# Down layer as seven block products (Strassen's scheme) in four chunks of inner rows

## What is computed

```python
def squared_relu_mlp(h, w_up, w_down):        # h 512x1024, w_up 1024x4096, w_down 4096x1024
    u = jax.nn.relu(h @ w_up)
    return (u * u) @ w_down
...
        h2 = _rms(x, norm2_g[l]).astype(dt)
        x = x + squared_relu_mlp(h2, w_up[l], w_down[l]).astype(dt)
    return x[:, BLOCK:]
```

## Time and profile before

| | us |
|---|---|
| median of 3 runs | 1192.71 (1192.49 to 1193.37) |
| the profiled execution | 1193.66 |
| its span in the trace | 1191.9 |
| PE busy | 1174.0 (98% of the span) |
| DVE, ACT, POOL busy | 499.2, 491.0, 468.1 |

### The profile page before, as it was taken

The page is one execution under the profiler, slowest core; times in us unless marked ns, Lnnn a source line. Parts: engine busy times, 40 slices in busy tenths (PEclk is TensorE's granted clock), DMA queues, the critical chain, the costliest instruction groups (busy, mean ns, idle before and its releaser), DMA issues.

```text
span 1191.9 us, 20669 instructions
## 1 busy us (share of the span) xinstructions
PE 1174.0 (98%) x8782; PEld 963.1 (81%) x8782; DVE 499.2 (42%) x994; ACT 491.0 (41%) x808; POOL 468.1 (39%) x288
## 2 busy tenths in 40 slices
PE   8999999999999999999999999999999999999998
PEld 7998877887798688667777777778888888888887
DVE  4699425454554643442452675262522000222000
ACT  6455423323323534765726544433634221343220
POOL 3443435335343234333323622343444544344541
PEclk9999999999999999999999999999999999999999
DMA  6222323122222152212522312342223332222330
GB/s 252 89 71 89 108 90 108 57 86 97 90 73 73 36 164 67 65 36 73 193 75 67 106 53 64 107 148 71 88 89 102 111 106 89 78 99 94 118 124 36
DMA packets 35998, 111.47 MB, mean 94 GB/s; under 512 B 4273, under 2 KB 9137, under 8 KB 35394
## 3 DMA queue, kind: packets, MB, share of 16 engines
q1 hardware_dynamic: 30288, 98.59, 24.9%
q10 hardware_dynamic: 5106, 11.43, 2.7%
q0 software_dynamic: 512, 0.13, 0.1%
HBM read 99.43 MB, written 9.04 MB: 91 GB/s over the span
## 4 chain that ended last, share of the span: by engine, by line
PE 83%; DVE 8%; ACT 4%; POOL 2%; issue 2%; DMA 0%; DVEq 0%; ACTq 0%
PE pst L1856 19%; PE pst L1858 18%; PE pst L1857 17%; PE pst L2032 5%; PE pst L2031 5%; PE pst L2030 5%; POOL w_lo L818 1%; PE pst L2371 1%; ACT w_hi L936 1%; PE pst L2363 1%; PE pst L2096 1%; PE pst L2149 1%; PE pst L2348 1%; PE pst L2333 1%; DVE cdif L1418 1%
## 5 line engine op out<-in xcount | busy, mean ns | idle before, releaser
L818 POOL TENSOR_TENSOR w_lo<-raw,w_hi 128x1024 fp32r<-128x1024 f32 x164 | 401.9, 2455 | 632.4 <-ACT w_hi L936 620.7
L1856 PE MATMUL pst<-h_hi,w_hi 128*128 128x512 f32 (+1 forms) x704 | 257.1, 365 | 1.3 <-DVE h_lo L1391 0.7
L1858 PE MATMUL pst<-h_hi,w_lo 128*128 128x512 f32 (+1 forms) x704 | 243.3, 346 | 0.0
L1857 PE MATMUL pst<-h_lo,w_hi 128*128 128x512 f32 (+1 forms) x704 | 242.9, 345 | 0.0
L936 ACT ACTIVATE w_hi<-raw 128x1024 fp32r<-128x1024 f32 x164 | 172.1, 1054 | 140.2 <-PE pst L2032 114.1
L1856 PEld LDWEIGHTS pst<-h_hi,w_hi 128*128 128x128 f32 x704 | 133.4, 189 | 25.9 <-issue 5.4
L1857 PEld LDWEIGHTS pst<-h_lo,w_hi 128*128 128x128 f32 x704 | 133.6, 190 | 15.7 <-issue 2.9
L1858 PEld LDWEIGHTS pst<-h_hi,w_lo 128*128 128x128 f32 x704 | 133.3, 189 | 15.9
L1856 PE MATMUL pst<-x_hi,w_hi 128*128 128x512 f32 (+1 forms) x272 | 102.6, 377 | 0.4 <-DVE x_lo L1722 0.4
L1857 PE MATMUL pst<-x_lo,w_hi 128*128 128x512 f32 (+1 forms) x272 | 102.4, 377 | 0.0
L1858 PE MATMUL pst<-x_hi,w_lo 128*128 128x512 f32 (+1 forms) x272 | 102.4, 376 | 0.0
(11 more groups left out here) (339 smaller groups left out, 1991.8 us busy)
## 6 DMA issues: line engine op xcount, KB each, us to landing
raw<-in_weights SPq DMA_DIRECT2D x164, 512.0 KB, 3.3
xt<-in_x SPq DMA_DIRECT2D x4, 512.0 KB, 5.4
wait_gate<-stage ACTq DMA_DIRECT2D x8, 256.0 KB, 2.0
gate_t<-wait_gate ACTq DMA_DIRECT2D x1, 2048.0 KB, 8.8
x<-in_x ACTq DMA_DIRECT2D x1, 2048.0 KB, 7.5
out<-x SPq DMA_DIRECT2D x7, 256.0 KB, 3.9
cst<-in_consts SPq DMA_DIRECT2D x1, 1524.0 KB, 11.3
wait_ret_g<-stage ACTq DMA_DIRECT2D x4, 256.0 KB, 2.2
```

The lines of the kernel that those rows point to most:

```text
L818: nc.gpsimd.tensor_tensor(w_lo[:, u % W_SLOTS, :], raw[:, u % RAW_SLOTS, :], w_hi[:, u % W_SLOTS, :].bitcast(F32), ALU.subtract).then_inc( ...
L1856: M(out, lh, rh, start=(first and i == 0), stop=False)
L1857: M(out, lh, rl, start=False, stop=False)
L1858: last = M(out, ll, rh, start=False, stop=(final and i == len(terms) - 1))
```

## The change

The inner rows are taken in four chunks of eight blocks of 128. In a chunk the down product is a 2x2 by 2x2 block product: the activations are split by tokens (two halves of 256) and by inner rows (two halves of four blocks), w_down's rows of the chunk likewise and its columns in two halves of 512. Seven products of such blocks are computed instead of eight, in the variant with shared partial sums (U11, U12, U22 and the sums S1 to S4 of the activations; four of the seven weight operands are differences). Each product is two jobs of one unit and 12 matmuls of 128x512 into two banks; three pairs of banks are used in turn.

- Units: 56 down units instead of 32; those of differences are raw blocks, loaded again. DVE subtracts another raw buffer from them in place (`weight_sums`, 8 per chunk) before ACT converts them; DVE does it ahead of its own step of an up or down job, for units up to five ahead of the job's. SP's load of a buffer also waits until the last such sum that reads it.
- Raw buffers: three more, so six, from the first up unit on; two lie in the space of constants no longer used.
- Up: ACT's relu goes to `usq`; DVE multiplies it by the relu of the PSUM bank (that empties the bank); ACT copies to `u_hi`, DVE subtracts to `u_lo`; behind each second job (the jobs pair block f with block f+4) DVE forms four sums of 128x256, ACT copies them in one go (128x1024), DVE makes their low parts (128x1024).
- Adding up: after each product DVE adds both banks to their places in `x2`; two of the products go to several quadrants, are collected in `shared` over the first three chunks, and are added to `x2` by `share_out` in the up stage of the last chunk.

In the diff, a line of "..." stands where lines are left out.

```diff
-JOBS = (PHASE_C + PHASE_A + PHASE_B + PHASE_D + PHASE_E + proj_jobs(BRANCH_SW) + PHASE_O + up_jobs(0) +
-        down_jobs(0) + up_jobs(1) + down_jobs(1))
+FC = 8
+NFC = DFF // P // FC
+UP_ORDER = [0, 4, 1, 5, 2, 6, 3, 7]
+TH = T // 2
+
+
+U11, U12, U22, S1, S2, S3, S4 = range(7)
+PRODUCTS = [("p11", U11, (0, 0)), ("p12", U12, (1, 0)), ("p51", S1, (0, 1)), ("p62", S2, (1, 1)),
+            ("p42", U22, (1, 0)), ("p73", S3, (0, 0)), ("p34", S4, (1, 1))]
+LESS = {2: 0, 3: 2, 4: 3, 5: 3}
+GOES_TO = [None, [(0, 0)], [(0, 1), (1, 1)], None, [(1, 0)], [(1, 0), (1, 1)], [(0, 1)]]
+NM = len(PRODUCTS)
+SHARED = {0: [(0, 0), (0, 1), (1, 0), (1, 1)], 3: [(0, 1), (1, 0), (1, 1)]}
+
+
+def up_jobs(c):
+    return [("up", c, i) for i in range(FC)]
+
+
+def down_jobs(c):
+    return [("down", c, (m, j)) for m in range(NM) for j in range(2)]
+
+
+JOBS = (PHASE_C + PHASE_A + PHASE_B + PHASE_D + PHASE_E + proj_jobs(BRANCH_SW) + PHASE_O +
+        [j for c in range(NFC) for j in up_jobs(c) + down_jobs(c)])
...
+        return u
+    (r, q), j = PRODUCTS[u[2][0]][2], u[2][1]
+    return "w_down", 4 * u[1] + 2 * r + j, q
...
+RAW_MORE = 3
+RAW_AT, RAW_FILL, _c = [], [], {}
+for _n in range(NU):
+    _i = (_n - FFN0) % (RAW_SLOTS + RAW_MORE)
+    RAW_AT.append(RAW_SLOTS + _i if _n >= FFN0 and _i < RAW_MORE else _n % RAW_SLOTS)
+    _c[RAW_AT[-1]] = _c.get(RAW_AT[-1], 1 if RAW_AT[-1] >= RAW_SLOTS else 0) + 1
+    RAW_FILL.append(_c[RAW_AT[-1]])
+LESS_UNIT = {UNIT_NO[("w_down", c, (m, j))]: UNIT_NO[("w_down", c, (LESS[m], j))]
+             for c in range(NFC) for m in LESS for j in range(2)}
+SUM_NO = {u: i for i, u in enumerate(sorted(LESS_UNIT))}
+LAST_SUM = {}
+for _u in sorted(LESS_UNIT):
+    LAST_SUM[LESS_UNIT[_u]] = SUM_NO[_u]
...
+        def down_bank(g, t):
+            return [(4, 5), (6, 7), (1, 3)][g % 3][t]
...
+        def operand_split(c, which, p):
+
+            return 3 * (FC // 2 * c + p) + (1 if which == U11 else 2 if which < S1 else 3)
...
             for u in range(RAW_SLOTS, NU):
-                sp.wait_ge(lo_ready, u - RAW_SLOTS + 1)
+                held = u - RAW_SLOTS if u < FFN0 + RAW_MORE else u - RAW_SLOTS - RAW_MORE
+                sp.wait_ge(lo_ready, held + 1)
+                if held in LAST_SUM:
+                    sp.wait_ge(raw_summed, KD + LAST_SUM[held] + 1)
...
-                    act.wait_ge(raw_in[u % RAW_SLOTS], 16 * (u // RAW_SLOTS + 1))
+                    act.wait_ge(*raw_loaded(u))
+                    if u in LESS_UNIT:
+                        act.wait_ge(*sums_done(u))
                     if u >= W_SLOTS:
                         act.wait_ge(dense_done, LAST_JOB[u - W_SLOTS] + 1)
-                    nc.scalar.activation(w_hi[:, u % W_SLOTS, :], raw[:, u % RAW_SLOTS, :], ACT.Copy)\
+                    nc.scalar.activation(w_hi[:, u % W_SLOTS, :], raw_unit(u), ACT.Copy)\
                         .then_inc(hi_ready, 1)
...
                 elif kind == "up":
-                    i = kind_no(n)
-                    if i >= 2:
-                        act.wait_ge(u_lo_ready, i - 1)
-                    A(ub[:, i % 2, :], one, ACT.Relu).then_inc(job_out[kind], 1)
+                    i, p, q = kind_no(n), b // 2, usq[:, b // 2 % 2, b % 2, :]
+                    act.wait_ge(dense_done, n + 1)
+                    if i >= 4:
+                        act.wait_ge(u_lo_ready, 3 * (i // 2 - 1))
+                    A(q, one, ACT.Relu).then_inc(u_hi_ready, 1)
                     act.wait_ge(job_out[kind], i + 1)
-                    if a == 1 and b == 0:
-                        act.wait_ge(dense_done, n)
-                    A(u_hi[:, b, :], ub[:, i % 2, :], ACT.Square).then_inc(u_hi_ready, 1)
+                    if b % 2 == 0:
+                        A(u_hi[:, p, U11, :], q[:, 0:TH], ACT.Copy).then_inc(u_hi_ready, 1)
+                    else:
+                        A(u_hi[:, p, U12:U22 + 1, :], halves(q), ACT.Copy).then_inc(u_hi_ready, 1)
+                        act.wait_ge(usum_ready, KD + i // 2 + 1)
+                        A(s_hi_[:, p], usum[:, p % 2], ACT.Copy).then_inc(u_hi_ready, 1)
                 after_job(n)
...
                 elif kind == "up":
-                    i = kind_no(n)
-                    r, q = ub[:, i % 2, :], usq[:, i % 2, :]
-                    dve.wait_ge(job_out[kind], i + 1)
-                    link(V.tensor_tensor(q, r, r, ALU.mult))
-                    dve.wait_ge(u_hi_ready, i + 1)
-                    V.tensor_tensor(u_lo[:, b, :], q, u_hi[:, b, :].bitcast(F32), ALU.subtract).then_inc(u_lo_ready, 1)
+                    i, p, par_ = kind_no(n), b // 2, b // 2 % 2
+                    weight_sums(UNIT_NO[units_of(JOBS[n])[0]] + RAW_SLOTS + RAW_MORE)
+                    q = usq[:, par_, b % 2, :]
+                    dve.wait_ge(u_hi_ready, 5 * (i // 2) + 2 * (b % 2) + 1)
+                    V.scalar_tensor_tensor(out=q, in0=one, scalar=0.0, in1=q, op0=ALU.max, op1=ALU.mult)\
+                        .then_inc(job_out[kind], 1)
+                    if b % 2 == 0:
+                        dve.wait_ge(job_out[kind], i + 1)
+                        dve.wait_ge(u_hi_ready, 5 * (i // 2) + 2)
+                        V.tensor_tensor(u_lo[:, p, U11, :], q[:, 0:TH], u_hi[:, p, U11, :].bitcast(F32), ALU.subtract)\
+                            .then_inc(u_lo_ready, 1)
+                    else:
+                        dve.wait_ge(job_out[kind], i + 1)
+                        u11, u21, u12, u22 = (usq[:, par_, k // 2, TH * (k % 2):TH * (k % 2) + TH] for k in range(4))
+                        sums = usum[:, par_]
+                        link(V.tensor_tensor(sums[:, 0], u21, u22, ALU.add))
+                        link(V.tensor_tensor(sums[:, 1], sums[:, 0], u11, ALU.subtract))
+                        V.tensor_tensor(sums[:, 2], u21, u11, ALU.subtract)
+                        V.tensor_tensor(sums[:, 3], u12, sums[:, 1], ALU.subtract).then_inc(usum_ready, 1)
+                        dve.wait_ge(u_hi_ready, 5 * (i // 2) + 4)
+                        V.tensor_tensor(u_lo[:, p, U12:U22 + 1, :], halves(q), u_hi[:, p, U12:U22 + 1, :].bitcast(F32),
+                                        ALU.subtract).then_inc(u_lo_ready, 1)
+                        dve.wait_ge(u_hi_ready, 5 * (i // 2) + 5)
+                        V.tensor_tensor(s_lo_[:, p], sums, s_hi_[:, p].bitcast(F32), ALU.subtract).then_inc(u_lo_ready, 1)
+                    if a == NFC - 1 and b in (1, 3):
+                        share_out(b // 2)
                 elif kind == "down":
-                    c, kk = b
+                    m, j = b
+                    weight_sums(UNIT_NO[units_of(JOBS[n])[0]] + RAW_SLOTS + RAW_MORE)
+                    if j == 0:
+                        return
+                    g = NM * a + m
+                    if g:
+                        dve.wait_ge(job_out["down"], g)
...
+                        (rq,) = GOES_TO[m]
+                        dve.wait_ge(rows_done, NB)
+                        dst = x2_part(rq, 0)
+                        V.tensor_tensor(dst, pst[:, down_bank(g, 0), :], dst, ALU.add).then_inc(job_out["down"], 1)
                         dve.wait_ge(dense_done, n + 1)
-                        for blk in range(NB):
-                            dst = x2[:, blk, T * c:T * c + T]
-                            V.tensor_tensor(dst, pst[:, down_bank(c, blk), :], dst, ALU.add)\
+                        for i in range(2):
+                            dst = x2_part(rq, 1)[:, 2 * P * i:2 * P * i + 2 * P]
+                            V.tensor_tensor(dst, pst[:, down_bank(g, 1), 2 * P * i:2 * P * i + 2 * P], dst, ALU.add)\
                                 .then_inc(job_out["down"], 1)
+                        return
+                    dve.wait_ge(dense_done, n + 1)
+                    for t in range(2):
+                        o = pst[:, down_bank(g, t), :]
+                        if m in SHARED and a < NFC - 1:
+                            e = shared[:, min(m, 1), t, :]
+                            last = V.tensor_tensor(e, o, e, ALU.add) if a else V.tensor_copy(e, o)
+                        else:
+                            for rq in GOES_TO[m] or SHARED[m]:
+                                last = V.tensor_tensor(x2_part(rq, t), o, x2_part(rq, t), ALU.add)
+                    last.then_inc(job_out["down"], 1)
+
+            summed = [0]
+
+            def weight_sums(upto_unit):
+                for v in range(max(summed[0], FFN0), min(upto_unit, NU)):
+                    if v in LESS_UNIT:
+                        less = LESS_UNIT[v]
+                        dve.wait_ge(*raw_loaded(v))
+                        dve.wait_ge(*(sums_done(less) if less in LESS_UNIT else raw_loaded(less)))
+                        V.tensor_tensor(raw_unit(v), raw_unit(v), raw_unit(less), ALU.subtract).then_inc(raw_summed, 1)
+                summed[0] = max(summed[0], upto_unit)
+
+            def share_out(t):
+
+                if t == 0:
```

(94 more changed lines are left out.)

48 lines of the change are left out of this document (22 added, 26 removed).

## The result

The changed kernel takes 1204.2 us (median of 4 runs, 1203.55 to 1204.72) against 1192.8: ratio 1.0095, 95% interval 1.0077 to 1.0112, so 11.4 us slower where 8.5 were forecast (1201.2). The profiled execution has a span of 1202.2 us against 1191.9.

What follows compares the result with a forecast made beforehand. PE was taken to bound the kernel. Saving 21.8 us against losses of 3 x 6.4, 7.6 and 3.5 gave +8.5 on the profiled 1193.66, so 1202.2; the median lies 0.95 lower, 1201.2 us, range 1191 to 1209.

Steps and rivals of the forecast that it cites:

- The saving: Down stages: 768 matmuls become 672, so 96 x 0.2267 = 21.8 us off PE.
- Rival 2: Down matmuls: each removed one is worth its 389 ns, 37.3 us in place of 21.8; total 1185.7; chance 0.02.
- Switch: From up to down: a chain of copies and sums delays w_lo of the third down unit, PE 2.5 us late.
- Alternation: Down stretch: weight sum and w_lo take turns, 3.33 us a pair against PE's 2.72; 6.4 us lost per chunk.
- small waits at every job behind d2: Down stage: after the third down job's wait, PE waits some 0.6 us at the next ones, none behind d11.
- Rival 1: Down stretch: sums and w_lo run side by side, so the saving stays; 1180.7 us; chance 0.10.
- rival 3: Down stretch: POOL goes first whenever both wait; 8.4 us lost per chunk, total 1209.6 us; chance 0.10.
- Last chunk: Last down stage: more additions of products 0 and 3 delay the sums; 7.6 us lost.
- Share-out: Last up stage: five SBUF additions delay emptying a bank, 1.0 us, then 2.5 us; together 3.5, bounds 0 and 5.
- DMA: Weight loads: 512 KB in 2.72 us is 193 GB/s; costed at nothing, with some 3 us of cover.
- The sum: Whole kernel: -21.8 + 3 x 6.4 + 7.6 + 3.5 = +8.5 us, giving 1201.2 us; chance 0.78.

Runs made afterwards that it cites:

- e8: Changed kernel with six converted-weight slots, share-out spread over four even jobs, and VectorE making difference units' w_lo four jobs ahead: 1177.38 us.
- e3: Changed kernel with ScalarE converting the next weight unit in each second up job before waiting for the four activation sums: 1205.0 us.
- e1: Changed kernel with each of the 32 weight sums on VectorE cut from 1024 to 8 columns: 1190.87 us.
- e2: Changed kernel with every weight sum done twice in a row: 1249.95 us.
- e9: Changed kernel with each weight sum replaced by a single-input VectorE reduction of the same 1024 columns: 1192.22 us.
- e4: Changed kernel with six converted-weight slots instead of four from the fifth up unit on, ScalarE and GpSimd five units ahead: 1190.71 us.
- e5: Changed kernel with the ten share-out additions of the last up stage spread over its four even jobs: 1201.06 us.

## Why the prediction held, point by point

- **The saving.** 96 matmuls at 0.2267 us, 21.8 us. The up stages of the changed kernel and the undisturbed down stages of e8 have that rate to the last digit. Rival 2 (389 ns each) is out.
- **Switch.** Forecast: w_lo of d2 at 7.55 behind the last up job, 2.5 us late. Measured: PE starts d2 at 890.64 - 882.95 = 7.7, 2.4 late. That it is part of the port's line and no loss of its own was not in the forecast's words; e3 showed it.
- **Alternation.** 3.33 us per sum and w_lo forecast, 3.35 measured. The sums of d6, d8, d10 and d11 end 12.0, 18.7, 25.4 and 31.1 us behind the last up job (the DVE rows above, less 882.95); forecast were 12.0, 18.6, 25.2 and 30.9. The forecast's small waits at every job behind d2 are there only at d6, d7 and d8 (0.5 each): at d3 to d5 the slow matmuls of the switch take their place. The sums' mean is 2.9 us and not 3.3, since those behind other VectorE work wait less (2.22), and POOL is busy for 89% of the first stage, not 80. Rival 1 (side by side) is out by e1, e2 and e9, rival 3 (POOL always first) by the sums' rows. The three stages lost 6.5 to 6.6 us against 6.4.
- **Last chunk.** Down 8.1 us against 7.6. Share-out gaps of 0.8 and 2.8 us (1.0 and 2.5 forecast), but 5.4 lost against 3.5: the term was mis-sized by the clock. Behind the gap of 2.8 us the matmuls start 0.43 apart and add 1.8 us here (in e1, e2 and e4 the clock did not fall there, and the stage is 1.5 us shorter, 47.4 to 47.5 against 49.0); the prediction did not cost a lower clock anywhere. At the four switches the same fall came and cost nothing in the changed kernel, being over before the port let d5 start: e5 has two down stages with it (44.67 and 44.65 us) and the third without it, 44.65, with waits of 0.5 from d3 to d8 in its place. That a term left out of the forecast cost nothing there is luck; in e9, where the port is free, it cost 1.7 us each time.
- **DMA.** Costed at nothing, with 3 us of cover for the last loads. No wait of PE leads back to a load; e8 ran at 201 GB/s. The load of d13 did come late for ScalarE, by 1.6 us, and its w_hi was there 35.9 us behind the last up job against 35.5 forecast, in time.
- **The sum.** 30.3 us of losses forecast, 33.2 measured; the 2.9 between are 1.9 in the last up stage (1.8 of them the clock), 0.5 in the last down stage and 0.5 in the other three together.

Open: why the lower clock followed most gaps of 2.4 to 2.8 us and not others of the same length (counted in the last section).
